# Half of layer one's modulation rows on TensorE, weight loads before the small constants, and chunk pairs in the out-projections of a six-layer network on one core

## What is computed

```python
cond = jax.nn.silu(c)
for i in range(DEPTH):
    shift, scale, gate = jnp.split(cond @ ada_w[i] + ada_b[i], 3, axis=-1)
    h = rmsnorm(x, norm_g[i]) * (1 + scale[:, None, :]) + shift[:, None, :]
    ...
    x = x + gate[:, None, :] * y
```

## Time and profile before

| what | us or share |
|---|---|
| median of 3 runs (lowest, highest) | 2681.12 (2678.57, 2683.32) |
| the profiled execution | 2680.32 |
| its span | 2678.5 |
| TensorE busy, weight loads busy | 2401.1 (90%), 1834.6 (68%) |
| VectorE busy | 1580.4 (59%) |
| ScalarE busy | 753.7 (28%) |
| GpSimd busy | 933.0 (35%) |
| granted TensorE clock, mean | 0.928 |

### The profile page before, as it was taken

One profiled execution on the slowest core, in us unless ns is written; L12 is line 12 of the kernel. 1 busy time (PEld: TensorE's weight loads), 2 busy tenths in 40 slices (PEclk: granted clock), 3 DMA queues, 4 the chain that ended last, 5 costly groups with the idle time before them and its releaser, 6 DMA issues.

```text
span 2678.5 us, 31421 instructions
## 1 busy us (share of the span) xinstructions
PE 2401.1 (90%) x12361; PEld 1834.6 (68%) x12361; DVE 1580.4 (59%) x2403; ACT 753.7 (28%) x1642; POOL 933.0 (35%) x944
## 2 busy tenths in 40 slices
PE   3969898979999999799969989999898998999987
PEld 2756677658887667677756866486577686658666
DVE  7686674754144565565664558583745446857373
ACT  2233201511001464234232143322401215232231
POOL 2885897479601456762120010401302001130030
PEclk6979898988788899899979999999998999999999
DMA  6440456044643001331111212131122121112111
GB/s 216 137 139 9 118 128 140 1 126 118 133 82 63 17 2 40 110 110 48 49 54 56 79 32 64 32 95 47 63 85 73 50 77 32 49 59 83 48 63 63
DMA packets 229158, 200.28 MB, mean 75 GB/s; under 512 B 86836, under 2 KB 213140, under 8 KB 228756
## 3 DMA queue, kind: packets, MB, share of 16 engines
q1 hardware_dynamic: 217491, 156.33, 21.1%
q0 software_dynamic: 11520, 41.95, 5.5%
HBM read 196.16 MB, written 2.10 MB: 74 GB/s over the span
## 4 chain that ended last, share of the span: by engine, by line
PE 59%; POOL 18%; DVE 15%; ACT 4%; issue 3%; DMA 0%; SPq 0%; DVEq 0%; ACTq 0%; POOLq 0%
PE bank L506 13%; PE bank L507 13%; PE bank L508 13%; POOL mix L2266 6%; PE bank L622 4%; POOL mix L2263 4%; PE bank L658 3%; PE bank L636 2%; POOL mix L2269 2%; POOL mix L2250 2%; DVE wring_parts L1517 2%; PE bank L822 2%; DVE qb L2005 1%; PE bank L572 1%; DVE bank L1618 1%
## 5 line engine op out<-in xcount | busy, mean ns | idle before, releaser
L507 PE MATMUL bank<-h_parts,whi_parts 128*128 128x512 f32 (+2 forms) x1336 | 541.5, 405 | 0.0
L1517 DVE TENSOR_TENSOR wring_parts<-wring,whi_parts 128x2048 fp32r<-128x2048 f32 (+2 forms) x126 | 306.0, 2428 | 4.3
L507 PEld LDWEIGHTS bank<-h_parts,whi_parts 128*128 128x128 f32 (+2 forms) x1336 | 254.4, 190 | 69.3 <-issue 5.9
L1516 DVE CAST whi_parts<-wring 128x2048 fp32r<-128x2048 f32 (+2 forms) x126 | 176.0, 1397 | 211.3 <-PE bank L508 169.3
L2266 POOL TENSOR_TENSOR mix<-mix 128x512 f32<-128x512 f32 (+1 forms) x160 | 217.1, 1357 | 12.5
L506 PE MATMUL bank<-vt_parts,whi_parts 128*128 128x512 f32 (+2 forms) x472 | 201.0, 426 | 18.0 <-POOL h_parts L2297 12.1
L507 PE MATMUL bank<-mix_parts,whi_parts 128*128 128x512 f32 x512 | 203.3, 397 | 0.0
L506 PE MATMUL bank<-pt_parts,whi_parts 128*128 128x512 f32 x392 | 165.4, 422 | 36.8 <-DVE wring_parts L1517 21.0
L508 PE MATMUL bank<-vt_parts,wring_parts 128*128 128x512 f32 (+2 forms) x472 | 190.9, 405 | 0.0
L2263 POOL TENSOR_TENSOR mix<-mix,cond 128x1024 f32<-128x1024 f32 x80 | 159.9, 1999 | 11.1 <-DMA mix<-in_ada_w 9.5
L1618 DVE CUSTOM_DVE_ANT_0 bank<-bank,causal 128x128 f32<-128x128 f32 (+3 forms) x256 | 120.4, 513 | 72.3 <-PE bank L622 71.8
(11 more groups left out here) (377 smaller groups left out, 5392.7 us busy)
## 6 DMA issues: line engine op xcount, KB each, us to landing
wring<-in_w_in SPq DMA_DIRECT2D x60, 1024.0 KB, 5.2
mix<-in_ada_w POOLq DMA_DIRECT2D x80, 512.0 KB, 4.8
wring<-in_w_out SPq DMA_DIRECT2D x16, 1024.0 KB, 4.9
wring<-in_mla_w_in SPq DMA_DIRECT2D x10, 1024.0 KB, 7.3
wring<-in_mla_w_out SPq DMA_DIRECT2D x8, 1024.0 KB, 5.0
wring<-in_swa_w_in SPq DMA_DIRECT2D x32, 256.0 KB, 4.9
wring<-in_nsa_w_in SPq DMA_DIRECT2D x32, 256.0 KB, 4.6
wring<-in_nsa_w_in SPq DMA_DIRECT2D x6, 1024.0 KB, 6.1
```

The source lines that it names most:

```text
L507: pe.matmul(bank, lh, rl, start=False, stop=False)
L1516: chain(dve.tensor_copy(high, whole))
L1517: dve.tensor_tensor(low, whole, high.bitcast(F32), ALU.subtract).then_inc(done, 1)
```

## The change

It has three parts. TensorE takes, for each of layer one's parts 0 and 1, the second 512 columns from the loaded weights themselves, in 32 products of a 128 by 128 block with one column of `cond`; the first 512 still come from DVE's sums and 4 products with ones. DVE makes the weighted rows of groups 0 and 2 alone. SP issues the first three weight units before the small constants. In the four layers of the first stack, the out-projection's first unit opens two banks and goes chunk by chunk through both blocks.

```diff
--- before.py
+++ after.py
@@ -586,7 +586,21 @@
 
                 n = 3 * L + part
 
-                pe.wait_ge(*(cnt(start_summed, 2) if n < 2 else cnt(ada_summed)))
+                if n < 2:
+                    bank = open_bank(V, ("ada", L, part))
+                    pe.wait_ge(start_loaded[2 * n + 1], 16 * len(start_ring[2 * n + 1]))
+                    pe.wait_ge(*cnt(cond_ready, 1 - n))
+                    for j in range(4):
+                        for k in range(KC):
+                            per = KC // len(start_ring[2 * n + 1])
+                            t = start_ring[2 * n + 1][k // per][:, k % per, :]
+                            pe.matmul(bank[:, 4 + j:5 + j], t[:, j * P:(j + 1) * P], cond[:, k:k + 1], start=(k == 0), stop=(k == KC - 1))
+                    pe.wait_ge(*cnt(start_summed))
+                    for j in range(4):
+                        mm = pe.matmul(bank[:, j:j + 1], acc[:, n, j * P:(j + 1) * P], ones[:, 0:1], start=True, stop=True)
+                    mm.then_inc(V.full, 1)
+                    return
+                pe.wait_ge(*cnt(ada_summed))
                 bank = open_bank(V, ("ada", L, part))
                 for j in range(8):
                     mm = pe.matmul(bank[:, j:j + 1], acc[:, n % 2, j * P:(j + 1) * P], ones[:, 0:1], start=True, stop=True)
@@ -661,12 +675,14 @@
             def out_proj(L, n_k, between=None, midway=None):
                 for i in range(4):
                     keys = [(L, "y", 2 * i + j) for j in range(2)]
-                    b = [open_bank(V, key) for key in keys] if n_k == 2 else None
+                    b = [open_bank(V, key) for key in keys] if n_k == 2 or i == 0 else None
                     for k in range(n_k):
                         slots = by_chunk(weights(L, ("out", i) if n_k == 1 else ("out", i, k)))
                         if between and i == 0 and k == n_k - 1:
                             between()
                         steps = [(j, c) for j in range(2) for c in range(KC)]
+                        if n_k == 1 and i == 0:
+                            steps = [(j, c) for c in range(KC) for j in range(2)]
                         if n_k == 2 and i == 0:
                             steps = [(j, c) for j in range(2) for c in range(4)] + [(j, c) for c in range(4, KC) for j in range(2)]
                         for j, c in steps:
@@ -1767,7 +1783,7 @@
                 if k:
                     add_square(0, k - 1)
             add_square(0, KC - 1)
-            for u in range(4):
+            for u in (0, 2):
                 weighted_rows(u)
             prepare(2)
 
@@ -2362,10 +2378,10 @@
                 for i, part in enumerate(parts):
                     per = KC // len(parts)
                     sp.dma_start(part, w[:, per * i:per * (i + 1), S * u:S * (u + 1)]).then_inc(start_loaded[u], 16)
-                if u == 3:
-                    load_small()
             for n, (_, make, _) in enumerate(units):
                 slot = n % W_SLOTS
+                if n == W_SLOTS:
+                    load_small()
                 if n >= W_SLOTS:
                     sp.wait_ge(*unit_done[n - W_SLOTS])
                 for to, of in make(W[slot]):
```

## The result

| | median, us | lowest to highest | runs |
|---|---|---|---|
| before | 2681.1 | 2676.6 to 2717.3 | 22 |
| after | 2700.7 | 2680.1 to 2716.1 | 22 |

The ratio is 1.0058 (95%: 1.0034 to 1.0081) in the paired comparison; the two medians are 19.5 us apart. The prediction was 2685.3 with a range of 2673 to 2690, so it is wrong: the changed kernel is slower by some 0.6 to 0.7%. The runs of one kernel don't lie around one value, but on levels. It reaches the old time, but seldom.

The account below looks back on a forecast made before the run. No single bound: TensorE carries 59% of the chain of waits, GpSimd 18%, DVE 15%. Terms +2.0 + 0 - 0 + 2.2 = +4.2 us took 2680.3 to 2684.5; with 0.8 to the median, 2685.3, range 2673 to 2690.

Parts of the forecast that it names:

- Part 1: Start: TensorE's 144 one-column records run at half clock, 0.215 us each, so layer one's input starts 2.0 us later.
- Rival B: Start: the clock rises under the one-column stream, input 9.8 us earlier, execution 2673.5 us; chance 0.14.
- Part 2: Start: weights ahead of small constants land soon after 36.9 us; worth nothing while TensorE sets the start, cost zero.
- Part 3: Layer one's out-projection ends 3.9 us earlier, all lost waiting for GpSimd; TensorE's wait grows from 2.90 to about 9.
- 2.2 us later: End of layer one: DVE's last split falls into GpSimd's last round and lengthens it by 2.2 us.
- 4.2: Whole execution: the sum of the terms, +4.2 us on the profiled 2680.3.
- The 2.0 us of the start: Start: layer one's input at 59.7 in place of 57.73 us, and layer one moves by as much.
- the last of the sum: Whole execution: the cost on the profiled execution plus 0.8 us to the runs' median gives 2685.3.
- the waits at the ends of layers two and three as before: Ends of layers two and three: TensorE's waits for GpSimd stay at 11.48 and 6.61 us.
- C: Ends of layers one to three: GpSimd pays in more places, 7.3 us in all, 2688.4; chance 0.18.

Follow-up runs that it names:

- e7: Kernel before, with GpSimd repeating its last sum four times ahead of layer two's attention; median 2712.9 us (4 runs).
- e9: Kernel before, with 20 unused bf16 products ahead of the first five steps' scores in layer two's attention; median 2684.1 us.
- e12: Kernel before, with GpSimd repeating its last sum seven times ahead of layer two's attention; median 2716.0 us (12 runs).
- e13: Kernel before, with ten unused f32 products in the wait ahead of layer two's attention and 20 bf16 at its first five steps; median 2693.9 us.
- e5: Kernel before, with ten unused f32 products of 512 columns in the wait ahead of layer two's attention; median 2709.3 us (seven runs).
- e17: Kernel before with e13's unused products, plus bf16 products behind the eight one-column products and ahead of every later attention step's scores; median 2684.9 us.
- e16: TensorE's rows and the weights ahead, without pairs, with the unused products of e13; median 2688.2 us.
- e2: Changed kernel without the out-projection's chunk pairs; median 2680.7 us (10 runs).
- e8: Kernel before with the pairs alone, and GpSimd repeating its last sum four times ahead of layer two's attention; median 2713.5 us.
- e11: Kernel before with the pairs alone, and 20 unused bf16 products ahead of the first five steps' scores in layer two's attention; median 2686.5 us.
- e15: Kernel before with the pairs alone, and the unused products of e13; median 2679.8 us, profiled run 2674.3.
- e4: Kernel before with the out-projection's chunk pairs alone; median 2712.8 us (4 runs), profiled run 2712.9.
- e3: Changed kernel with DVE making all weighted rows, so weights and pairs only; median 2711.4 us (8 runs).
- e1: The changed kernel itself, all parts, run again; median 2702.5 us (6 runs), profiled run 2702.0.
- e14: Changed kernel with the unused products of e13; median 2690.7 us.
- e18: Changed kernel with the unused products of e17; median 2687.2 us.
- e6: Changed kernel with ten unused f32 products of 512 columns in the wait ahead of layer two's attention; median 2706.1 us (twelve runs).
- e10: Changed kernel with 20 unused bf16 products ahead of the first five steps' scores in layer two's attention; median 2688.1 us.

## Why the prediction was wrong, and where it was right

**Part 1, right.** The stream of one-column products went at half clock: 144 records in 30.7 us are 0.213 each (taken: 0.215), and the input came 1.9 us later (2.0). Rival B, from which the range has its lower end, is out. The Trainium skill ("TensorE: Matmul & The Clock Gate", Part 1: The HAM clock gate) lets sustained activity release the clock; 30 us of it did not here, at one column for each weight load.

**Part 2, right in the sum, not in its reason.** The weights went out at 22.50 and still DVE waited 1.84 and 0.82 us for them: in the median their transfers took 8.5 to 14.6 us to land, by size, where they took 7.0 to 9.4 before. They now run while the last rows come in, and between 24 and 36 us the core moves 386 to 389 GB/s in both kernels; that the two share this rate is the likely cause, not a tested one. The 10.89 us of idle time behind hid that.

**Part 3, right in place, too large in size.** The wait for the chunk is gone, and so is the half clock behind it. Against the profile of before the out-projection did win 4.0 us: it began 4.1 later than before (DVE's first cast for it at 268.09 against 263.99), and its last residual came 0.14 later (311.90 against 311.76). All of it was lost at GpSimd, as foreseen. But the last round grew by 0.9, not by 2.2, and TensorE's wait became 6.54, not 9, chiefly since the out-projection began 4.1 us later and not 2.0. The profile of before also misleads about the gain: of the nine profiles with the old order only it and e7's have the wait of 2.1 us and the half clock behind it. The other seven wait 0.52 to 0.55 us, as e9 does, so that there the pairs have little to win:

```profile
269.53 0.50 PE L506 MATMUL bank<-qb_parts,whi_parts 128*128 128x512 f32 x1 [0.55 <-DVE mix_parts L1549]
```

For the price the profiles must be paired by one more thing that the first two hide: the half clock ahead of layer one's attention is some 6 us long (195 to 201) in one half of the kernels' profiles and 13 (190 to 203) in the other, whatever the kernel. By the table below that is worth 1.1 to 1.8 us. Before had the short one, the changed kernel's first profile the long one. TensorE's restart at the end of layer one in all twenty profiles, us:

| | short | long |
|---|---|---|
| rows and order as before | 314.1 to 314.6 (before, e9, e12, e13) | 316.0 to 316.4 (e5, e7, e17) |
| rows and weights, no pairs | none | 316.6, 318.2 (e16, e2) |
| pairs alone | 315.6, 316.1 (e8, e11) | 316.9, 317.6 (e15, e4) |
| weights and pairs | 316.4 (e3) | none |
| all of the change | 317.5 to 318.0 (e1, e14, e18) | 318.4 to 319.2 (after, e6, e10) |

Two of the rows of this table, e9's and e11's, both of the short kind; the wait is 3.83 with the old order and 6.42 with the new:

```profile
314.39 3.57 PE L592 MATMUL bank<-ones,mix 128*128 128x1 f32 x16 [3.83 <-POOL mix L2273]
```

```profile
316.13 3.57 PE L592 MATMUL bank<-ones,mix 128*128 128x1 f32 x16 [6.42 <-POOL mix L2275]
```

Of the 1.7 us between these two, half lies in GpSimd's last round (5.24 and 6.12 us long) and half ahead of it, as its start shows, in e9 and then in e11:

```profile
309.10 1.91 POOL L2267 TENSOR_TENSOR mix<-mix,cond 128x1024 f32<-128x1024 f32 x1
```

```profile
309.96 1.91 POOL L2269 TENSOR_TENSOR mix<-mix,cond 128x1024 f32<-128x1024 f32 x1
```

So, by the middles of the groups, the pairs cost 1.1 (long) to 1.5 us (short) there and the whole change 2.6 to 3.3. The term "2.2 us later" was too large by about 1, and the agreement of 4.3 with 4.2 is partly luck: 1.1 to 1.8 of the 4.3 is the longer half clock. The 2.0 us of the start don't all arrive at this place either: with the rows and without the pairs it is 0.4 (e16) to 2.0 us (e2) later than with neither.

**The step that failed** is the last of the sum: "The median of the runs is 2681.1, 0.8 above it, so I predict 2685.3". It carries the cost through layers two to six as if nothing there depended on when it happens. Its sign "the waits at the ends of layers two and three as before" was true (11.47, 6.61; in e1 10.71, 6.64), and yet layer two's attention ahead of them is 19 us longer in e1's profile, and 21 of the changed kernel's 28 runs lie 11 to 32 us above the time of its first. The rows to suspect it were to be had. Windows of the kernel before:

```profile
440.00:460.00 20.00, 10.77 (x62) 9.68 (x61) 2.78 (x7) 1.08 (x2) 13.78 (x14) 0.68 0.65 149
460.00:480.00 20.00, 19.62 (x148) 14.70 (x148) 10.58 (x43) 8.71 (x34) 7.17 (x14) 0.64 0.01 2
480.00:500.00 20.00, 15.79 (x170) 11.68 (x168) 18.16 (x55) 9.69 (x36) 8.61 (x16) 1.00 0.00 1
```

A wait of 8.8 us, then 20 us at a mean of 0.64 with TensorE busy for 19.62 of them, then full clock: half clock from 447 to 474, and work that fills TensorE for 12 us before it rises. I read the granted clock only in the three places that the change touches, and at 454 to 458, just ahead of this attention, where the earlier trace rows has it at 0.50 and I took it for the price of a record alone. None of the rivals names this attention; C, the only one that ends above the forecast, has GpSimd for its cause. The three runs shown before lay within 5 us of each other, and I took that for the spread; 26 of 153 runs are 30 us above.

**What the runs show, and what not.** Shown: the levels are the attention's clock (all twenty profiles have the attention's length by its clock, those of e9 to e11 and e13 to e18 with their added products besides, and the execution by the attention to within 10 us); the pairs alone, or 2.1 us more of waiting in the kernel before, put it on the upper level; 20 unused products at the attention's start take most of the loss away. Not shown: why a given start is good or bad. The Trainium skill (the same page and section) says that the moment at which the clock rises varies from run to run with where the kernel's start falls; it also has "the ramp penalty is <1% of a typical kernel span", and here this one stretch makes 33 us, 1.2% (e4 against before), since it lasted the attention's whole 102 us. That the placement of the attention against such moments decides is in keeping with e1 and e7, while e8 and e12 didn't come out as this theory expected; it stays an argument. In particular it isn't shown how the pairs' 1.1 to 1.5 us, or their order of work, lead to a bad start. Open too is what share of the changed kernel's loss TensorE's rows add.

## What to carry to other kernels

A cost of 4 us has two parts: the work itself, and what the shift does to a later stretch in which the clock can rise early or stay down. Go through the granted clock of the whole profile, also where the change touches nothing, and mark stretches that enter at 0.50, fill TensorE, and rise only after 10 us or more; there a change of 2 us can cost 30, and the range must hold it. And run such a kernel ten times or more before its spread is believed.

## What was unexpected of the hardware

- 32 attention steps of small products, identical and with the first six reciprocals at the same distances to 0.01 us (12.0 in all), ran at half clock for their first 12 us in one execution (after) and for all of their 102 in another (e4). The last four steps take 13.8 us at half clock (e4) and 7.9 at full (before).
- A busy TensorE doesn't keep its clock: it fell at 459 (e5), behind 8.8 us of dense products and 3 us of one-column products and small scores, and at 498 (e10) in the attention itself.
- Unused products can be worth their time: 20 of bf16 took 26 us off the median of e4's kernel. Ten of f32 in the wait ahead instead (e5) raised that of the kernel before by 30.
